# The first model's projections and attention as one loop: a projected unit and one head per step

## The reference

```
h = rms_norm(x, ln1_gain[l]);  proj = h @ w_in[l]
nsa_q(6 heads x 64), k/v_cmp, k/v_slc, k/v_win (2 groups x 64 each), nsa_gate,
  mla_cq(256), mla_ckv(128), mla_kpe(32), ret_q, ret_k, ret_v, ret_gate (5 x 64) = split(proj)
# 1  rotary on nsa_q, k_cmp, k_slc, k_win; masked softmax attention of 6 heads over k_slc and
#    over k_win; and over 15 compressed keys: gelu(32-token blocks @ w1) @ w2; sum of the three by sigmoid gates
# 2  mla: q = rms_norm(cq) @ w_uq, (k, v) = rms_norm(ckv) @ w_ukv, rotary on 32 dims; 5 heads of causal attention
# 3  retention, 5 heads: (q k^T * decay) @ v, group norm, times silu(ret_gate)
x = x + concat(1, 2, 3) @ w_out[l]
x = x + square(relu(rms_norm(x, ln2_gain[l]) @ w_up[l])) @ w_down[l]
```

## Time and profile before

| | us |
|---|---|
| median of 3 runs | 1707.88 (1705.79 to 1711.88) |
| the profiled execution: its own time, its span | 1703.29, 1701.5 |
| TensorE busy in the span | 1590.1 (93%) |
| VectorE busy, ScalarE busy | 1121.3 (66%), 784.8 (46%) |
| share of TensorE in the chain that ended last | 80% |

### The profile page before, as it was taken

The page is one execution under the profiler, slowest core; times in us unless marked ns, Lnnn a source line. Parts: engine busy times, 40 slices in busy tenths (PEclk is TensorE's granted clock), DMA queues, the critical chain, the costliest instruction groups (busy, mean ns, idle before and its releaser), DMA issues.

```text
span 1701.5 us, 28687 instructions
## 1 busy us (share of the span) xinstructions
PE 1590.1 (93%) x11878; PEld 1517.9 (89%) x11878; DVE 1121.3 (66%) x1904; ACT 784.8 (46%) x1369; POOL 59.5 (3%) x61
## 2 busy tenths in 40 slices
PE   5998879999899888999989997899998998889999
PEld 4986779999898667999989997899998998889999
DVE  6836567877773556878888556665557844666653
ACT  4533347743443234774344544444435454354442
POOL 0000000000000000000003003000000300300000
PEclk9977579999897757999999999999999999999999
DMA  6420047889542004788954443355553434335452
GB/s 272 169 104 25 1 149 247 312 310 352 190 174 100 25 1 148 264 312 324 340 194 152 147 152 133 115 202 195 175 193 128 160 122 183 125 130 199 174 197 75
DMA packets 41889, 296.51 MB, mean 174 GB/s; under 512 B 4640, under 2 KB 4768, under 8 KB 6304
## 3 DMA queue, kind: packets, MB, share of 16 engines
q1 hardware_dynamic: 41184, 293.31, 47.3%
q10 hardware_dynamic: 576, 1.37, 0.2%
HBM read 293.61 MB, written 1.05 MB: 173 GB/s over the span
## 4 chain that ended last, share of the span: by engine, by line
PE 80%; DVE 10%; ACT 3%; DMA 3%; issue 2%; POOL 1%; ACTq 0%; DVEq 0%
PE acc L748 22%; PE acc L750 22%; PE acc L749 22%; DVE wL L1465 3%; DMA ring<-stream 3%; PE ps_s L839 2%; ACT wH L1183 2%; PE ps_t L846 1%; PE ps_s L838 1%; PE acc L915 1%; PE acc L823 1%; PE ps_o L856 1%; PE ps_o L855 1%; PE acc L996 1%; POOL region L2076 1%
## 5 line engine op out<-in xcount | busy, mean ns | idle before, releaser
L1465 DVE TENSOR_TENSOR wL<-ring,wH 128x1024 fp32r<-128x1024 f32 x444 | 547.5, 1241 | 272.8 <-ACT wH L1183 270.2
L748 PE MATMUL acc<-hH,wH 128*128 128x256 f32 x2368 | 691.6, 292 | 35.6 <-DVE hL L1474 21.6
L749 PE MATMUL acc<-hL,wH 128*128 128x256 f32 x2368 | 679.7, 287 | 0.0
L750 PE MATMUL acc<-hH,wL 128*128 128x256 f32 x2368 | 679.3, 287 | 0.0
L1183 ACT ACTIVATE wH<-ring 128x1024 fp32r<-128x1024 f32 x444 | 463.2, 1050 | 222.2 <-PE acc L750 136.2
L748 PEld LDWEIGHTS acc<-hH,wH 128*128 128x128 f32 x2368 | 464.9, 196 | 46.0 <-issue 39.3
L749 PEld LDWEIGHTS acc<-hL,wH 128*128 128x128 f32 x2368 | 465.0, 196 | 3.3 <-issue 2.9
L750 PEld LDWEIGHTS acc<-hH,wL 128*128 128x128 f32 x2368 | 464.4, 196 | 0.0
L748 PE MATMUL acc<-aH,wH 128*128 128x256 f32 x864 | 244.7, 283 | 0.1
L749 PE MATMUL acc<-aL,wH 128*128 128x256 f32 x864 | 244.5, 283 | 0.0
L750 PE MATMUL acc<-aH,wL 128*128 128x256 f32 x864 | 244.5, 283 | 0.0
(11 more groups left out here) (308 smaller groups left out, 1731.1 us busy)
## 6 DMA issues: line engine op xcount, KB each, us to landing
ring<-stream SPq DMA_DIRECT2D x276, 1024.0 KB, 4.8
cst<-consts SPq DMA_DIRECT2D x1, 1411.0 KB, 14.9
x<-xin SPq DMA_DIRECT2D x4, 256.0 KB, 5.4
out<-x SPq DMA_DIRECT2D x4, 256.0 KB, 4.1
onc<-once ACTq DMA_DIRECT2D x1, 516.0 KB, 9.4
v1all<-vec ACTq DMA_DIRECT2D x1, 371.0 KB, 7.0
v2all<-vec SPq DMA_DIRECT2D x1, 330.0 KB, 19.1
nv<-pos ACTq DMA_DIRECT2D x1, 256.0 KB, 4.3
```

The lines of the kernel that those rows point to most:

```text
L748: pe.matmul(out, w[0], y[0], start=first, stop=False)
L749: pe.matmul(out, w[0], y[1], start=False, stop=False)
L750: return pe.matmul(out, w[1], y[0], start=False, stop=last)
L1465: TTN(wL[:, n % SPLIT, :], ring[:, g % RING, half * UNIT:(half + 1) * UNIT], wH[:, n % SPLIT, :].bitcast(F32), ALU.subtract).then_inc(lo_r ...
```

## The change

The two stages become one. The three latent units (cq0, cq1, ckv) are projected first, side by side; then q0, ks, q1, the latents' sums of squares as one step (ssqk), and tm0. Then come 19 slots. Slot i has one projected unit (FILL1, in slots 0 to 15), head i's scores, the transposes of head i-1 and the values of head i-2, and behind them what END1 names. The rotation of an already projected unit stands in the middle of the slot's unit (MID1). The heads' order is by query unit (0, 3, 1, 4, 2, 5), the tiles of the stream are ordered as they are used, SBUF places are shared otherwise. The transposes mt0 to mt4 stand in slots 16 to 18, before the last head is done, the other three behind; the first three output units are projected side by side, chunk by chunk. One VectorE instruction with a broadcast scales a head's output in place of two (slc and mla heads, and the 8 heads of the second model).

```diff
-UNITS1 = ["q0", "q1", "q2", "ks", "kw", "kc", "vc", "cq0", "cq1", "ckv", "kpe", "rqa", "rqb", "rka", "rkb", "r4"]
-ROPED1 = ["q0", "q1", "q2", "ks", "kw", "kc", "kpe", "rqa", "rqb", "rka", "rkb", "r4"]
+UNITS1 = ["cq0", "cq1", "ckv", "q0", "ks", "q1", "kc", "q2", "kw", "vc", "kpe", "rqa", "rka", "rqb", "rkb", "r4"]
+RAW1 = {u: 6 + i if i < 3 else (i - 3) % 6 for i, u in enumerate(UNITS1)}
...
+PAIRS1 = [(UNITS1[2 * i], UNITS1[2 * i + 1]) for i in range(8)]
 TILES1 = (
-    [(UNITS1[2 * i], UNITS1[2 * i + 1]) for i in range(8)]
-    + [("tm", j) for j in range(4)]
-    + [("cmpk", 0), ("cmpv", 0), ("small", 0)]
+    PAIRS1[0:3] + [("tm", 0), ("tm", 1), PAIRS1[3], ("cmpk", 0)] + PAIRS1[4:6] + [("cmpv", 0), ("small", 0)]
+    + PAIRS1[6:8] + [("tm", 2), ("tm", 3)]
...
-HEADS1 = [("slc", h) for h in range(NSA_HEADS)] + [("win", h) for h in range(NSA_HEADS)] \
-    + [("mla", h) for h in range(MLA_HEADS)]
+BY_QUERY = [h for r in range(REP) for h in (r, REP + r)]
+HEADS1 = [(kind, h) for kind in ("slc", "win") for h in BY_QUERY] + [("mla", h) for h in range(MLA_HEADS)]
...
-def behind1(i):
-    steps = {
-        0: ["hidk"],
-        1: ["hidv", "mq0"],
-        2: ["mq1", "rot_mq0", "mk0", "mk1"],
...
+FILL1 = ["tm10", "tm11", "kc", "q2", "kw", "vc", "kpe", "rqa", "rka", "rqb", "rkb", "r4", "tm20", "tm21", "tm30", "tm31"]
+SLOTS1 = NH1 + 2
+MID1 = {3: ["kc"], 4: ["q2"], 5: ["kw"], 7: ["kpe"], 8: ["rqa"], 9: ["rka", "mq0"], 10: ["rqb", "mq1"],
+        11: ["rkb", "mq2"], 12: ["r4", "mq3"], 13: ["mq4"]}
+ROPES1 = ["q0", "ks", "q1"] + [u for i in range(SLOTS1) for u in MID1.get(i, [])]
+END1 = {4: ["hidk"], 6: ["mk0", "mk1", "mk2"], 7: ["hidv", "mk3", "mk4"], 8: ["mv0", "mv1", "mq0"], 9: ["mq1", "mq2"],
+        10: ["kcc", "mq3", "mq4", "vbd"], 11: ["cs0", "cs1"], 12: ["rs0", "rs1"],
+        13: ["ct", "ro0", "ro1", "rs2", "rs3"], 14: ["co0", "co1", "ro2", "ro3", "rs4"], 15: ["ro4"],
+        16: ["mt0", "mt1"], 17: ["mt2"], 18: ["mt3", "mt4"]}
+EARLY_MIXED = 5
+def fill1(i):
+    return FILL1[i] if i < len(FILL1) else None
+def fed_by(i):
+    done = UNITS1[:6] + ["tm00", "tm01"] + FILL1[:i]
+    n = SPLIT
+    while n - SPLIT < 24 and SU1[n - SPLIT][2] in done:
+        n += 1
+    return min(n, 22) if i == 11 else n
...
+            def project_tokens(kind, j, t, n, mid=None):
+                if t == 0:
+                    state["parts"] = [[v.rearrange("p (c n) -> p c n", n=256) for v in next_unit()] for _ in range(2)]
+                parts = state["parts"]
+                a = open_acc(f"{kind}{j}{t}")
+                for c in range(KC):
+                    if mid is not None and c == KC // 2:
+                        mid()
+                    wh, wl = (v[:, c % 4, 0:n] for v in parts[c // 4])
+                    hh, hl = hH[:, c, t * P:(t + 1) * P], hL[:, c, t * P:(t + 1) * P]
+                    last = split_product(a[:, 0:n], (hh, hl), (wh, wl), c == 0, c == KC - 1)
+                last.then_inc(acc_full, 1)
...
+                project_side_by_side(UNITS1[:SIDE], normed(0))
+                if L == 0:
+                    pe.wait_ge(early_in, 16 * 3)
+                project("q0", hs)
+                project("ks", hs, mid=lambda: rotated("q0"))
+                project("q1", hs, mid=lambda: rotated("ks"))
+                latent_squares()
+                project_tokens("tm", 0, 0, TM_W[0], mid=lambda: rotated("q1"))
+                project_tokens("tm", 0, 1, TM_W[0])
+                if L == 0:
+                    pe.wait_ge(late_in, 16 * 3)
+                drained("tm00")
+                drained("tm01")
+                for i in range(SLOTS1):
+                    u = fill1(i)
+                    if u is None:
+                        middle(i)
+                    elif u[:2] == "tm":
+                        project_tokens("tm", int(u[2]), int(u[3]), TM_W[int(u[2])], mid=lambda: middle(i))
+                    else:
+                        project(u, hs, mid=lambda: middle(i))
+                    if i < NH1:
+                        kind, hh = HEADS1[i]
+                        if kind == "mla":
+                            roped(f"mq{hh}")
+                            if hh == 0:
+                                pe.wait_ge(km_ready, L + 1)
+                        else:
+                            roped(f"q{hh % REP}")
+                            roped("ks" if kind == "slc" else "kw")
+                        scores(head1, i, NH1, 0, L)
+                    if 1 <= i <= NH1:
+                        weights_transposed(i - 1, NH1, 0, L)
+                    if i >= 2:
+                        values(head1, i - 2, NH1, 0, L)
+                    after(i)
+                for c in range(EARLY_MIXED, KC):
+                    transposed(c)
+                project_side_by_side([f"wo{n}" for n in range(SIDE)], lambda c: drained(f"mt{c}"))
...
+                for i, u in enumerate(UNITS1[:SIDE]):
+                    take(A1, u, L, raw[:, RAW1[u], :])
+                    act.wait_ge(acc_drained[A1.bank(u)], A1.drained(u, L))
+                    act.activation(latsq3[:, i, :], raw[:, RAW1[u], :], ACT.Square).then_inc(latsq, 1)
+                feed(SIDE + SPLIT)
+                for i, u in enumerate(("q0", "ks", "q1")):
+                    take(A1, u, L, raw[:, RAW1[u], :])
+                    feed(SIDE + SPLIT + i + 1)
+                act.wait_ge(acc_drained[A1.bank("ssqk")], A1.drained("ssqk", L))
+                act.activation(ny[:], nv[:], ROOT).then_inc(y_ready, 1)
+                if L == 0:
+                    sines(slice(1, 4))
...
+                for i in range(SLOTS1):
+                    feed(fed_by(i))
+                    if fill1(i):
+                        taken(fill1(i))
+                    if (L, i) == (0, 1):
+                        act.wait_ge(late_in, 16 * 3)
+                        act.activation(ada_t, cb2, ACT.Tanh, scale=0.5).then_inc(ctanh, 1)
+                    if 1 <= i <= NH1:
+                        transposed_copy(i - 1, NH1, 0, L)
+                    taken_after(i)
+                    if i == 8:
+                        act.wait_ge(ge, L * 2 + 1)
+                        act.activation(gel[:, 1, 0:60], gel[:, 1, 0:60], ACT.Exp, scale=-2.0 * GELU_C).then_inc(ge, 1)
+                    if i == 12:
+                        act.wait_ge(csub, L + 1)
+                        act.activation(pc[:], pc[:], ACT.Exp).then_inc(cexp, 1)
+                    if i < NH1:
+                        exponentials(i, NH1, 0, L)
+                    if i == NH1 - 1:
                         act.wait_ge(gn_v, L + 1)
                         act.activation(gnst[:, 3, :], gnst[:, 2, :], ROOT).then_inc(gn_y, 1)
...
+                angles = iter(range(10)) if L == 0 else iter(())
+                def angles_on(n):
+                    for step in itertools.islice(angles, n):
+                        angle(step, 1, 4)
+                feed(SIDE + SPLIT)
+                angles_on(3)
+                feed(SIDE + SPLIT + 1)
+                if L == 0:
+                    dve.wait_ge(trig_ready, 2)
+                rope1_block("q0")
+                angles_on(2)
+                feed(SIDE + SPLIT + 2)
+                rope1_block("ks")
+                feed(SIDE + SPLIT + 3)
+                a = full(A1, "ssqk", L)
+                TSC(nv[:, 0, :], a[:, 0:S], 1.0 / 256, EPS, ALU.mult, ALU.add)
+                TSC(nv[:, 1, :], a[:, S:2 * S], 1.0 / 128, EPS, ALU.mult, ALU.add).then_inc(acc_drained[A1.bank("ssqk")], 1)
+                angles_on(5)
                 dve.wait_ge(y_ready, L * Y1 + 2)
...
+                    if kind != "win":
+                        at = 64 * hh + (384 if kind == "mla" else 0)
+                        last = TTN(mixed[:, :, at:at + 64], ps_o[:, 0:2 * HD].rearrange("p (t d) -> p t d", t=TT),
+                                   coef[:, i, :].unsqueeze(2).to_broadcast([P, TT, HD]), ALU.mult)
+                    else:
+                        for t in range(TT):
                             m = mixed[:, t, 64 * hh:64 * hh + 64]
-                            last = STT(m, o, coef[:, i, t:t + 1], m, ALU.mult, ALU.add)
+                            last = STT(m, ps_o[:, 64 * t:64 * t + 64], coef[:, i, t:t + 1], m, ALU.mult, ALU.add)
...
+                for i in range(SLOTS1):
+                    if i == 2:
+                        gates_squashed()
+                    if (L, i) == (0, 3):
+                        dve.wait_ge(ctanh, 1)
+                        link(STT(cb2, ada_t, 1.0, cb2, ALU.add, ALU.mult))
+                    if i == 7:
+                        dve.wait_ge(trig_ready, 4)
+                    for u in MID1.get(i, []):
+                        rope1_block(u)
+                    if i == 6:
+                        dve.wait_ge(acc_drained[A1.bank("vc")], A1.drained("vc", L))
+                        shifted(raw[:, RAW1["vc"], :], 1)
+                    feed(fed_by(i))
                     if i < NH1:
```

(31 more changed lines are left out.)

436 lines of the change are left out of this document (168 added, 268 removed).

## The result

The changed kernel takes 1647.39 us (median of 4 runs, 1646.14 to 1650.70) against 1708.38 us before: ratio 0.9645, 95% interval 0.9622 to 0.9667. Forecast was 1660 in a range of 1630 to 1693. The profiled execution took 1646.14 us; its span is 57.1 us shorter (1701.5 to 1644.4).

What follows compares the result with a forecast made beforehand. The attention loop was held bound by TensorE at 1.2 GHz, hand-offs a smaller part. Gains of 25.0 (layer 1) and 22.3 us (layer 0), 47.3, take the profiled 1703.29 to 1656.0; forecast median 1660, range 1630 to 1693.

Steps and rivals of the forecast that it cites:

- Start: Layer's stretch before slot 0: 29.5 us in layer 1; layer 0 6.3 more, as ScalarE takes tm00 and tm01 behind the sines.
- Slots, work and waits: Slots 0 to 15 of layer 1: 108.8 us of work at full clock plus 7.5 us of waits.
- The 3.5 us at slot 0: Slot 0: VectorE's queue behind the sums of squares delays head 0's maxima, so TensorE gets its transposes 3.5 us late.
- The wait for q2: Slot 4: head 4's scores wait for q2's rotation, which VectorE reaches some 3 us late.
- The clock's term: Slots 4, 7, 13 and 14: the clock falls behind each one's unit, 2.2 us lost per fall, 8.8 us per layer.
- Rival A: Slots: the clock stays full throughout, saving 2 x 8.8 us more, kernel 1643 us; chance 0.15.
- Tail: Slots 16 to 18, without units: 15.5 us, of which VectorE's work is 12.2 us, then three transposes and waits.
- The stream's new order: Weight stream: reordered tiles cost nothing, as a tile serves two slots and the DMA engines are 0.24 busy.
- One scaling instead of two, output units side by side: Both attentions and the output projections: neither counted as a cost; the output units up to 1 us per layer if not.
- Rival B: Slots: hand-offs cost 1.13 us in each of 16, 18 us instead of 7.5 per layer, kernel 1681 us; chance 0.24.
- C: Slots: the clock does not come back within a unit, +92 us per layer, kernel 1844 us; chance 0.05.
- D: Layers of the first model: nothing is gained, since in-order VectorE, 70% busy in 170 us, is the new bound; chance 0.03.

Runs made afterwards that it cites:

- e10: Changed kernel with the old end: all eight mixed-column transposes behind the last slot, first three output units projected in turn; 1653.07 us, ratio 0.9678.
- joined kernel: Changed kernel with four edits: new stream order, layer 0's angles early, last head's masking before splits, hidk's preparation behind q2's rotation; 1630.16 us, ratio 0.9549.
- e4: Changed kernel with slot 16's copies and splits of the next weight units behind the last head's masking and exponentials; 1650.63 us, ratio 0.9668.
- e6: Changed kernel with VectorE masking the last head before slot 16's splits, and wo3's copy and split behind the last mixed column; 1648.70 us, ratio 0.9636.
- e1: Changed kernel with the projected unit of each of slots 0 to 15 cut to 3 of its 24 matmuls; 1635.54 us, ratio 0.9601.
- e7: Changed kernel with eight of the 16 narrow matmuls of hidk and of hidv moved into the middle of the next slot's unit; 1650.36 us, ratio 0.9666.
- the six executions: Changed kernel measured twice plus four edited kernels that leave its slots as they are; layer 0's slots took 114.6 to 121.5 us.

## Why the prediction was right, and where not

The mechanism was right: the clock comes back between small products, and it is most of the gain. The sum was 10 us too high for the profiled execution (1656.0 against 1646.14). The slots, forecast at 125.1 us in layer 1 and by the same terms at 125.3 in layer 0, came out 6.0 and 7.7 us shorter, layer 0's start 1.8 shorter, the two tails 3.4 longer each. These errors partly cancel, so the total is better than its terms.

- **Start.** Layer 1: 29.5 forecast, 29.7 measured; the new wait for ks's unit is 1.0 us where I put 1.8. Layer 0: 6.3 more than layer 1 forecast, 4.3 measured (34.04 less 29.72).
- **Slots, work and waits.** 108.8 + 7.5 + 8.8 = 125.1 forecast, 119.1 and 117.6 measured. The most mis-sized term is the waits: 7.5 forecast, 3.8 and 3.5 us of idle time measured. What is left of the difference, 2 to 4 us, is work and clock. The 3.5 us at slot 0 did not occur at all: head 0's transposes stand in slot 1, behind tm11's unit, and I had them in slot 0. The wait for q2 is 1.0 us in layer 1 and 2.3 in layer 0, not 3. Instead came 2.7 us behind the stream in layer 1.
- **The clock's term.** 8.8 per layer forecast; 115.34 x 0.07 = 8.1 and 114.06 x 0.06 = 6.8 measured. The size was right in these two, with 0.93 and 0.94 in the slots where the prediction put 0.85 to 0.9; since layer 0's same slots cost 117.42 x 0.11 = 12.9 in e10's execution, that closeness is partly luck. Half of the places were wrong: the clock is down at slot 4 in layer 0 or 6 in layer 1, at 7 and behind 11, not at 13 and 14, where retention stands. Rival A did not come. The Trainium skill (TensorE: Matmul & The Clock Gate, "HAM oscillation — how this bites in real kernels") ties the fall to gaps in which the engine has nothing to do. The windows 82.60 to 92.70 and 487.80 to 495.80 leave that open, since waits of 2.29 and 2.65 us stand ahead of them. 502.00 to 509.00 and 539.50 to 543.50 speak against it, since TensorE is busy in all of them and no wait but those listed above stands in these slots. In the joined kernel TensorE idles 0.8 us in the 110.3 of layer 0's slots, no gap over 0.4, and the clock is 0.95.
- **Tail.** 15.5 forecast, 18.9 measured. The step that failed is "VectorE makes ... 12.2 us": it left out the two splits that slot 16 still feeds (2.36 us) and the 2.06 us that VectorE waits for ScalarE to round them:

```profile
569.86 2.36 DVE L1543 TENSOR_TENSOR wL<-ring,wH 128x1024 fp32r<-128x1024 f32 x2 [2.06 <-ACT wH L1230]
```

The runs e4 and e6 show that chain from both sides.
- **"The stream's new order" costs nothing.** Wrong. I looked at the two tiles for tm2 and tm3 and at the DMA engines' load. What held up the stream was the place of a tile that a late reader frees, and the order of one queue behind it. It cost 2.65 us of waiting in layer 1, by luck offset by the 3.5 at slot 0, and a fall of the clock behind it, 7.24 x 0.43 = 3.1 us by estimate.
- **One scaling instead of two, output units side by side**: at most 1 us, as said. No run tried the scaling alone.
- Rival B (1.13 us per slot) is refuted by the same idle times in sixteen slots; C and D by the result. B's idea has a share in another sense: e1 shows that the units cover 11 to 14 us of hand-offs per layer. Two small slips in the rivals' arithmetic change nothing: A comes to 1642, and D's share of VectorE to 67% (114.24 of 170).

## What to carry to other kernels

Where a trace shows small matmuls running at 1.2 GHz, try putting large ones that are needed anyway between them before trimming either: here they bought some 26 us of clock per layer, and even useless matmuls were half repaid. After such an interleaving, look at in-order queues: which engine's chain ends the part without units, and which buffer is held by the latest reader. Run the same program more than once, and learn which of its stages repeat. The wait that TensorE names need not be the one that binds; follow the engine that has no idle time.

## What the runs showed of the hardware

The clock falls at different slots in two executions of one kernel: 0.94 and 0.93 in the slots of layers 0 and 1, then 0.91 and 0.95, with the same waits to 0.3 us. Over the six executions of the same slots it moved layer 0 by 7 us and layer 1 by 3, as much as most single edits here or more, so their price is read from the stages that repeat.

The clock also falls while TensorE has no wait. In the joined kernel's slots these are all the falls, two per layer:

```profile
77.00:84.00 7.00, 7.00 (x34) 0.51 0.22 68
135.00:139.00 4.00, 4.00 (x19) 0.57 0.30 127
466.00:470.00 4.00, 4.00 (x22) 0.57 0.41 133
520.00:524.00 4.00, 4.00 (x26) 0.60 0.56 231
```

TensorE is busy throughout each. The first and third begin while it works through hidk, products of 30 columns (75.56 to 81.2 and 462.96 to 467.0); the second and fourth while it works through the compressed scores, products of 16 columns (133.0 to 135.6 and 518.8 to 521.4). hidv, with 30 columns too, had no fall in this execution, nor had retention or the mla products. That the narrow products are the cause is not shown: the one run meant for it, e7, lengthened a wait as well.
